# Routed experts of a two-block model: 127 blocks of 128 slots as split fp32r products, and 80 blocks of four quarters with an expert each as plain float32

## The chip, the cores and the metric

The kernel runs on one core of a Trainium2 chip. Its time is device microseconds (us) of one execution, launch to end; three executions of the kernel before stand behind the median below. TensorE (PE) multiplies, VectorE (DVE), ScalarE (ACT) and GpSimd (POOL) compute beside it, SyncE (SP) issues most DMAs. All data are float32; fp32r is a format that TensorE reads faster than float32 and that keeps fewer bits, so the kernel before splits operands into a high and a low part.

## The reference

Two blocks are computed one after the other: `first_block` (modulation, projection, two recurrent mixers, output projection, a mixture of experts) and `second_block`. What the change touches is the mixture of experts of the first block, for 1024 tokens of 1024 numbers, 64 experts of inner width 256, of which every token takes 8:

```python
def _swiglu(x, wg, wu, wd):
    return (jax.nn.silu(x @ wg) * (x @ wu)) @ wd

def _moe(h, router_w, router_b, wg, wu, wd, sg, su, sd):
    ...
    _, top_e = lax.top_k(sel, TOP_K)
    gate = jnp.take_along_axis(scores, top_e, axis=1)
    gate = gate / jnp.sum(gate, axis=-1, keepdims=True) * ROUTE_SCALE
    ...
    def step(out, inp):
        tok, gw, e = inp
        y = _swiglu(h[tok], wg[e], wu[e], wd[e]) * gw[:, None].astype(h.dtype)
        return out.at[tok].add(y), None
    routed, _ = lax.scan(step, jnp.zeros_like(h), (tok_buf, gate_buf, blk_e))
    return _swiglu(h, sg, su, sd) + routed
```

The result is `x = x + g2 * _moe(h2_lat)`, normalized; the second block starts from it.

## The kernel before

The program is a row of stages, each with one block of instructions for every engine. Four of them matter here, in this order.

**`output_route`** (about 1530 to 1740 us) multiplies by `w_out` in 8 tiles of 128 tokens, normalizes, and computes router scores and gates. Every token's row with its 64 gates is stored to `yn` in HBM. SyncE issues the stores of a tile in the loop around L1960.

**`shared_expert`** counts the choices of each expert, and gives each expert as many blocks of 128 slots as it needs. A table in HBM holds the token of each slot; L2295 fetches it, 128 slots to a partition, and it is turned into `slots`. `owner` holds the expert of each block, and `done`, for each expert, where its blocks start. The shared expert's result is stored to `total` in HBM.

**`routed_experts`** (1800 to 3097 us) takes 127 blocks (`USED`), as many as could be needed. Block j, expert e:
- GpSimd gathers the 128 token rows of block j+3 into `xg` (L2494) and scatters the result of block j-1 with an addition into `total` (L2503). A scatter waits for the one before it.
- TensorE turns the rows of block j+1 (8 transposes, L2526), multiplies block j by the gate and up weights of its expert (8 slices of 128 rows, each 512 columns, three fp32r products for each: high x high, high x low, low x high, L2559), then multiplies block j-1 by its down weights (`down`: 6 fp32r products L2541, 2 plain float32 ones L2542), then transposes the hidden values of block j (L2568).
- ScalarE makes the high parts of the weights (`w_high`, 4 of 128x1024 a block, L2585; `wd_high`, L2605) and of the rows (L2580), the silu (L2623), and the scaled result (L2610).
- VectorE makes the low parts by subtraction (L2649, L2656, L2643), the product `hid` (L2683), and the indices.
- SyncE loads an expert's gate and up weights (L2468, two DMAs of 1 MB into `exp_w`, a ring of 4 experts) when the expert four back in the ring has been split for the last time, and its down weights (L2472, 1 MB into `wd`, also a ring of 4) when that expert's last down product is done. All three loads of an expert stand in one row of the queue, three experts ahead of use:

```python
with sp.Fori(1, N_EXPERTS // WS) as i:
    for w in range(WS):
        blocks = sp.value_load(tb["done"][0:1, bass.ds(i * WS + (w - WS + 1), 1)], ...)
        sp.wait_ge(w_split, blocks * Q)
        first(i * WS + w, w)
        sp.wait_ge(y_ready, blocks + 1)
        second(i * WS + w, w)
```

The order on each engine is the order of the code; the first four blocks and the last three are written out, the rest is a loop of four blocks. Semaphores count steps.

**The first stage of the second block** (`pre_...`, from 3107 us) loads each of 8 tiles of `total` and of x (L3438, L3441), multiplies `total` by the gain (L3655), adds it to x (L3667), normalizes twice, and transposes the tile on TensorE (L3523); then it multiplies by its projection weights (L3510). SyncE stores the tile (L3473) and loads small parameters between the tiles (L3459, L3463).

## Time and profile before

| | us |
|---|---|
| median of 3 executions | 4236.89 |
| lowest and highest | 4229.92, 4244.08 |
| the profiled execution | 4234.69 |
| its span, first to last instruction | 4232.8 |

| engine | busy us | share of the span |
|---|---|---|
| TensorE, products | 3643.4 | 86% |
| TensorE, loads of the stationary operand | 2938.0 | 69% |
| VectorE | 2676.3 | 63% |
| ScalarE | 2044.4 | 48% |
| GpSimd | 907.3 | 21% |

The shares are means over stages with different limits. The largest groups are all in the routed experts: VectorE's subtraction for `w_low` (603.0 us in 512 instructions), ScalarE's rounding for `w_high` (510.9 us) and TensorE's three kinds of product (415.0, 404.1 and 404.0 us). TensorE's instructions overlap and their ends are modelled, so a period is read from start to start, not from busy times. The DMA queues moved 690.96 MB. The chain of waits that ended last covers only the final stage, 4% of the span, so it says nothing of the stages spoken of here.

### The profile page before, as it was taken

To read this page: it belongs to the slowest core of one execution; us is meant where nothing else is said; L and a number is where in the kernel's file an instruction comes from. 1 tells how busy PE (TensorE), PEld (TensorE's weight loads), DVE (VectorE), ACT (ScalarE), POOL (GpSimd) and SP (SyncE) were. 2 spreads that over 40 slices of the span, in tenths; PEclk is the share of its full clock that TensorE was granted. 3 is DMA by queue.
4 is the path that set the end of the run, shared out by engine and by line. 5 is a ranking of instruction groups with operands and counts; after the bars stand their busy time and mean duration, and the time that the engine had idled before them with its cause. 6 is when DMAs were issued, how large, how long until landed. Compare 5 with 4: busy or idle time off the path is not lost. (4 is left out here: it accounts for less than half of the span.)

```text
span 4232.8 us, 93615 instructions
## 1 busy us (share of the span) xinstructions
PE 3643.4 (86%) x35448; PEld 2938.0 (69%) x35449; DVE 2676.3 (63%) x4120; ACT 2044.4 (48%) x2837; POOL 907.3 (21%) x799
## 2 busy tenths in 40 slices
PE   4899799678776679799999999999949989968779
PEld 0898788577676557377777677777737767856667
DVE  2588688555555566287777777777768666036731
ACT  1477576322222153077777777777742222136720
POOL 3000000134433003323223233322213333300000
PEclk6899899799899789899999999999969999989989
DMA  8254344322210635499999999754563421355552
GB/s 302 76 172 155 116 159 153 128 68 56 81 54 9 216 136 138 154 318 270 277 342 341 341 338 340 190 108 108 111 168 90 119 75 60 110 139 134 131 169 80
DMA packets 527112, 690.96 MB, mean 163 GB/s; under 512 B 77904, under 2 KB 424656, under 8 KB 523728
## 3 DMA queue, kind: packets, MB, share of 16 engines
q1 hardware_dynamic: 487232, 545.70, 40.5%
q0 software_dynamic: 39088, 139.12, 13.4%
q8 instruction: 240, 3.93, 0.4%
q10 hardware_dynamic: 480, 1.62, 0.1%
q14 instruction: 72, 0.59, 0.0%
HBM read 508.35 MB, written 178.00 MB: 162 GB/s over the span
## 5 line engine op out<-in xcount | busy, mean ns | idle before, releaser
L2649 DVE TENSOR_TENSOR routed_w_low<-moe_exp_w,routed_w_high 128x1024 fp32r<-128x1024 f32 x512 | 603.0, 1219 | 26.8 <-ACT routed_w_high L2585 23.5
L2585 ACT CAST routed_w_high<-moe_exp_w 128x1024 fp32r x512 | 510.9, 1045 | 61.7 <-DMA moe_exp_w<-in_exp_w_up_dram 26.0
L2503 POOL DMA_INDIRECT total<-routed_y,routed_yidx x127 | 238.0, 1874 | 825.6 <-ACT routed_y L2610 304.4
L2559 PE MATMUL routed_p_gu<-routed_w_high,routed_x_high 128*128 128x512 f32 x1016 | 415.0, 408 | 0.0
L2559 PE MATMUL routed_p_gu<-routed_w_low,routed_x_high 128*128 128x512 f32 x1016 | 404.1, 398 | 0.0
L2559 PE MATMUL routed_p_gu<-routed_w_high,routed_x_low 128*128 128x512 f32 x1016 | 404.0, 398 | 0.0
L548 PE MATMUL front_ps<-front_a_high,front_w_high 128*128 128x320 f32 (+1 forms) x1120 | 363.5, 325 | 16.7 <-DVE front_w_low L785 13.5
L548 PE MATMUL front_ps<-front_a_high,front_w_low 128*128 128x320 f32 (+1 forms) x1120 | 355.2, 317 | 0.0
L548 PE MATMUL front_ps<-front_a_low,front_w_high 128*128 128x320 f32 (+1 forms) x1120 | 355.0, 317 | 0.0
L3510 PE MATMUL pre_ps<-pre_a_high,pre_w_high 128*128 128x512 f32 x720 | 287.7, 400 | 15.3 <-ACT pre_xb L3644 6.6
L3510 PE MATMUL pre_ps<-pre_a_low,pre_w_high 128*128 128x512 f32 x720 | 281.7, 391 | 0.0
L3510 PE MATMUL pre_ps<-pre_a_high,pre_w_low 128*128 128x512 f32 x720 | 281.7, 391 | 0.0
L2542 PE MATMUL routed_p_y<-routed_wd,routed_hT_rest 128*128 x508 | 260.2, 593 | 0.0
L1427 POOL TENSOR_TENSOR rwmix_TT<-rwmix_at,rw_mask 64x256 f32<-64x256 f32 (+1 forms) x60 | 43.4, 724 | 944.4 <-DVE rwmix_at L1328 938.5
L548 PEld LDWEIGHTS front_ps<-front_a_high,front_w_high 128*128 128x128 f32 x1120 | 214.3, 191 | 35.5 <-DVE front_w_low L785 18.1
L2559 PEld LDWEIGHTS routed_p_gu<-routed_w_high,routed_x_low 128*128 128x128 f32 x1016 | 192.1, 189 | 46.7
L2559 PEld LDWEIGHTS routed_p_gu<-routed_w_low,routed_x_high 128*128 128x128 f32 x1016 | 192.9, 190 | 41.0
L2559 PEld LDWEIGHTS routed_p_gu<-routed_w_high,routed_x_high 128*128 128x128 f32 x1016 | 192.9, 190 | 41.1
L548 PEld LDWEIGHTS front_ps<-front_a_low,front_w_high 128*128 128x128 f32 x1120 | 214.2, 191 | 1.3
L548 PEld LDWEIGHTS front_ps<-front_a_high,front_w_low 128*128 128x128 f32 x1120 | 213.9, 191 | 0.0
L2494 POOL DMA_INDIRECT moe_xg<-yn,moe_idx x128 | 157.8, 1233 | 104.5 <-DVE moe_idx L2638 53.7
L3510 PEld LDWEIGHTS pre_ps<-pre_a_high,pre_w_high 128*128 128x128 f32 x720 | 136.2, 189 | 48.7 <-issue 18.1
(556 smaller groups left out, 8362.3 us busy)
## 6 DMA issues: line engine op xcount, KB each, us to landing
moe_exp_w<-in_exp_w_gate_dram SPq DMA_DIRECT2D x64, 1024.0 KB, 14.4
moe_exp_w<-in_exp_w_up_dram SPq DMA_DIRECT2D x64, 1024.0 KB, 19.3
routed_wd<-in_exp_w_down_dram SPq DMA_DIRECT2D x64, 1024.0 KB, 15.5
front_wt<-in_w_in_dram SPq DMA_DIRECT2D x70, 512.0 KB, 4.3
mod_w<-in_w_mod_dram SPq DMA_DIRECT2D x24, 1024.0 KB, 18.1
pre_wt<-in_w_in_dram SPq DMA_DIRECT2D x44, 512.0 KB, 4.1
out_a<-mix SPq DMA_DIRECT2D x24, 512.0 KB, 4.4
proj<-pre_xv SPq DMA_DIRECT2D x16, 512.0 KB, 2.6
```

What stands on the lines that cost most here:

```text
L548: op = nc.tensor.matmul(ps[:, s % 2, c, 0:size], w_part[:, s % 2, k, :], a_part[:, k, first + c * size:first + (c + 1) * size], start=(k = ...
L1427: nc.gpsimd.tensor_tensor(combos(TT[u][:])[to, es], combos(at[u][:])[at_rows, es], mask(MASK_LEVEL, at_rows, es), ALU.mult)
L2494: nc.gpsimd.indirect_dma_start(xg[:, b % 2, :], None, yn, bass.IndirectOffsetOnAxis(ap=idx[b][:, :], axis=0))\
L2503: nc.gpsimd.indirect_dma_start(total, bass.IndirectOffsetOnAxis(ap=yidx[b % 2][:, :], axis=0), y[:, b % 2, :], None, compute_op=ALU.add).t ...
L2542: op = nc.tensor.matmul(p_y[:, h, :], hT_rest[:, :], wd[:, bass.ds(e % WS, 1), 1, cols], start=False, stop=True)
L2559: op = nc.tensor.matmul(p_gu[:, :], x_part, w_part[:, k, :], start=(k == 0 and i == 0), stop=(k == KD - 1 and i == 2))
L2585: nc.scalar.copy(w_high[:, q * KQ:(q + 1) * KQ, :].rearrange("p k m -> p (k m)"), wgu[:, bass.ds(e % WS, 1), q * KQ:(q + 1) * KQ].rearrang ...
L2649: nc.vector.tensor_tensor(w_low[:, at, :].rearrange("p k m -> p (k m)"), wgu[:, bass.ds(e % WS, 1), at].rearrange("p o k j m -> p (o k j m)"),
L3510: op = nc.tensor.matmul(ps[:, u, a:a + n], w_part[:, u, k, :], a_part[:, k, a:a + n], start=(k == 0 and j == 0), stop=(k == KD - 1 and j = ...
```

## The change

A block becomes a quad of four quarters (`QUARTER` = 32 slots); each quarter has an expert of its own (`owner` has an entry for each of the four places of a quad), and there are 80 quads (`QUADS`), as many as could be needed.

- TensorE multiplies in plain float32. For each slice of weights four matmuls stand in a row, one for each quarter: 32 columns of the rows as stationary operand, 512 columns of that quarter's expert's weights moving, the output in partitions 32s to 32s+31 of one PSUM bank (L2590 up, 8 groups; L2605 down, 4 groups). The first quarter reads the weights from the ring by a register; the others read from `fixed`, a ring of 4 places.
- ScalarE copies the second quarter's weights into `fixed` (6 copies of 128x1024 a quad), VectorE those of the third and fourth (12 copies). The roundings and subtractions go.
- Each quarter adds into a copy of `total` of its own: `total` has four parts of `PART` rows. The shared expert's result is in part 0; the other three are filled with zeros by SyncE in `output_route`.
- SyncE's order: `next_first` of expert e+3 waits for the last quad's up products of expert e-1, and `next_second` of expert e stands behind it.
- `shared_expert` computes four owners for each quad with four times as wide a comparison, 4 transposes and 4 gathers of the table where there was 1.
- The first stage of the second block loads four parts for each tile (`sums_of`), TensorE adds them as products with the identity into a PSUM bank (8 plain float32 products a tile), and VectorE multiplies by the gain from there (2 instructions of 128x512).

```diff
+                if 1 <= i < SPOTS:
+                    sp.dma_start(total[i * PART:i * PART + SEQ, :].rearrange("(p r) (a l) -> p (r a) l", p=P, l=P),
+                                 none[:].rearrange("p (o l) -> p o l", o=1).broadcast_to([P, SEQ * D // P // P, P])).then_inc(none_sent, 16)
...
-BLOCKS = SEQ * TOP_K // P + N_EXPERTS
-USED = (SEQ * TOP_K + (P - 1) * N_EXPERTS + N_EXPERTS - TOP_K) // P
+SPOTS = 4
+QUARTER = P // SPOTS
+QUADS = (SEQ * TOP_K + (QUARTER - 1) * N_EXPERTS + N_EXPERTS - TOP_K) // QUARTER // SPOTS + 1
+PART = SEQ + QUARTER
...
-            nc.gpsimd.indirect_dma_start(places[:, :], None, table.rearrange("(b l) c -> b (l c)", l=P),
-                                         bass.IndirectOffsetOnAxis(ap=row[:, :], axis=0)).then_inc(fetched, 16)
+            for j in range(SPOTS):
+                nc.gpsimd.indirect_dma_start(places[:, j * QUARTER:(j + 1) * QUARTER], None, table.rearrange("(b l) c -> b (l c)", l=QUARTER),
+                                             bass.IndirectOffsetOnAxis(ap=row[:, j:j + 1], axis=0)).then_inc(fetched, 16)
...
-        wgu = tb["exp_wgu"]
+        wgu = tb["exp_rows"]
         wd = st.sb("wd", [P, WS, MT, D])
-        w_high, w_low = (st.sb(n, [P, KD, 2 * D_EXPERT], F32R) for n in ("w_high", "w_low"))
+        fixed = st.sb("fixed", [P, R, SPOTS - 1, D])
         gate = st.sb("gate", [P, BS])
         idx = tb["idx"]
         yidx = [st.sb(f"yidx{u}", [P, 1], U32) for u in range(2)]
         xg = tb["xg"]
-        x_high, x_low = (st.sb(n, [P, 2, KD, P], F32R) for n in ("x_high", "x_low"))
+        x = st.sb("x", [P, 2, KD, P])
...
+        def up_step(j, c):
+            return j * STEP + c
+
+        def down_step(j, m):
+            return NB * STEP + m if ends(j) else j * STEP + (STEP + CH + m)
+
+        def place_of(b, c):
+            return (b * STEP + c) % R
+
+        def spot(s):
+            return slice(s * P // SPOTS, (s + 1) * P // SPOTS)
...
+            def next_first(e, at, w):
+                quad = sp.value_load(tb["done"][0:1, at], min_val=0, max_val=NB - 2)
+                sp.wait_ge(chunk_done, quad * STEP + CH)
+                first(e, w)
+
+            def next_second(e, at, w):
+                quad = sp.value_load(tb["done"][0:1, at], min_val=0, max_val=NB - 2)
+                sp.wait_ge(chunk_done, quad * STEP + 2 * STEP)
+                second(e, w)
+
+            def only(e):
+                return bass.ds(e, 1)
 
             for w in range(WS):
                 if w:
                     sp.sem_inc(second_loaded[w], 16)
                 second(w, w)
-            with sp.Fori(1, N_EXPERTS // WS) as i:
+            for e in range(WS, 2 * WS - 1):
+                next_first(e, only(e - WS + 1), e % WS)
+            with sp.Fori(1, N_EXPERTS // WS - 1) as i:
                 for w in range(WS):
-                    blocks = sp.value_load(tb["done"][0:1, bass.ds(i * WS + (w - WS + 1), 1)], min_val=1, max_val=NB)
-                    sp.wait_ge(w_split, blocks * Q)
-                    first(i * WS + w, w)
-                    sp.wait_ge(y_ready, blocks + 1)
-                    second(i * WS + w, w)
+                    next_first(i * WS + (w + WS - 1), only(i * WS + w), (w + WS - 1) % WS)
+                    next_second(i * WS + w, only(i * WS + (w - WS + 1)), w)
+            for e in range(N_EXPERTS - WS, N_EXPERTS):
+                if e + WS - 1 < N_EXPERTS:
+                    next_first(e + WS - 1, only(e), (e + WS - 1) % WS)
+                next_second(e, only(e - WS + 1), e % WS)
...
+            def copies(g):
+                pe.wait_ge(first_copied, g + 1)
+                pe.wait_ge(others_copied, g + 1)
+
+            def up(j, b):
+                e = owner(pe, j, 0)
+                pe.wait_ge(x_made, j + 1)
+                if not begins(j):
+                    pe.wait_ge(hid_made, j)
+                for c in range(CH):
+                    copies(up_step(j, c))
+                    for k in range(c * KC, (c + 1) * KC):
+                        cols = slice((k - c * KC) * BANK, (k - c * KC + 1) * BANK)
+                        for s in range(SPOTS):
+                            w = wgu[:, bass.ds(e % WS, 1), k * BANK:(k + 1) * BANK] if s == 0 else fixed[:, place_of(b, c), s - 1, cols]
+                            op = nc.tensor.matmul(p_gu[spot(s), :], x[:, b % 2, k, spot(s)], w, start=(k == 0), stop=(k == KD - 1))
+                    op.then_inc(chunk_done, 3 if begins(j) and c == CH - 1 else 1)
+
+            def down(j, b):
+                e = owner(pe, j, 0)
+                pe.wait_ge(hT_made, j + 1)
+                if not begins(j):
                     pe.wait_ge(y_made, j)
-                for h in range(2):
-                    cols = slice(h * BANK, (h + 1) * BANK)
-                    for i, (h_part, w_part) in enumerate(((hT_high, wd_high), (hT_high, wd_low), (hT_low, wd_high))):
-                        nc.tensor.matmul(p_y[:, h, :], h_part[:, :], w_part[:, cols], start=(i == 0), stop=False)
-                    op = nc.tensor.matmul(p_y[:, h, :], hT_rest[:, :], wd[:, bass.ds(e % WS, 1), 1, cols], start=False, stop=True)
-                op.then_inc(y_ready, 1)
-
-            pe.sem_inc(y_ready, 1)
+                for m in range(MT):
+                    copies(down_step(j, m))
+                    at = place_of(0, m) if ends(j) else place_of(b + 1, CH + m)
+                    for h in range(2):
+                        cols = slice(h * BANK, (h + 1) * BANK)
+                        for s in range(SPOTS):
+                            w = wd[:, bass.ds(e % WS, 1), m, cols] if s == 0 else fixed[:, at, s - 1, cols]
+                            op = nc.tensor.matmul(p_y[spot(s), h, :], hT[:, m, spot(s)], w, start=(m == 0), stop=(m == MT - 1))
+                    op.then_inc(chunk_done, 1)
+
...
+                if not ends(j):
+                    turn(j + 1, (b + 1) % BS, r + (b + 1) // BS)
+                up(j, b)
+                if not begins(j):
+                    down(j - 1, (b - 1) % BS)
...
+            def up_copy(e, j, b, c):
+                g = up_step(j, c)
+                if not isinstance(j, int) or g >= R:
+                    act.wait_ge(chunk_done, g - (R - 1))
+                nc.scalar.copy(fixed[:, place_of(b, c), 0, :],
+                               wgu[:, bass.ds(e % WS, 1), c * D:(c + 1) * D].rearrange("p o n -> p (o n)"))\
+                    .then_inc(first_copied, 3 if begins(j) and c == CH - 1 else 1)
+
+            def down_copies(j, b):
+                e, last = owner(act, j, 1), owner(act, j, SPOTS - 1)
                 for w in range(WS):
-                    act.wait_ge(second_loaded[w], (e + (WS - w)) // WS * 16 + (16 if w else 0))
-                if not isinstance(j, int) or j >= 1:
-                    act.wait_ge(y_ready, j + 1)
-                nc.scalar.copy(wd_high[:, :], wd[:, bass.ds(e % WS, 1), 0, :].rearrange("p o n -> p (o n)")).then_inc(down_rounded, 1)
+                    act.wait_ge(second_loaded[w], (last + (WS - w)) // WS * 16 + (16 if w else 0))
+                for m in range(MT):
+                    act.wait_ge(chunk_done, down_step(j, m) - (R - 1))
...
+            def up_copies(es, j, b, c):
+                g = up_step(j, c)
+                if c == 0:
+                    for w in range(WS):
+                        dve.wait_ge(loaded[w], (es[-1] + (WS - w)) // WS * 32 + (16 if w else 0))
+                if not isinstance(j, int) or g >= R:
+                    dve.wait_ge(chunk_done, g - (R - 1))
+                for s in (2, 3):
+                    op = nc.vector.tensor_copy(fixed[:, place_of(b, c), s - 1, :],
+                                               wgu[:, bass.ds(es[s] % WS, 1), c * D:(c + 1) * D].rearrange("p o n -> p (o n)"))
+                op.then_inc(others_copied, 3 if begins(j) and c == CH - 1 else 1)
+
+            def down_copies(j, b):
+                es = owner(dve, j, 2), owner(dve, j, 3)
+                for w in range(WS):
+                    dve.wait_ge(second_loaded[w], (es[1] + (WS - w)) // WS * 16 + (16 if w else 0))
+                for m in range(MT):
+                    dve.wait_ge(chunk_done, down_step(j, m) - (R - 1))
+                    at = place_of(0, m) if ends(j) else place_of(b + 1, CH + m)
+                    for s, e in zip((2, 3), es):
+                        op = nc.vector.tensor_copy(fixed[:, at, s - 1, :], wd[:, bass.ds(e % WS, 1), m, :].rearrange("p o n -> p (o n)"))
+                    op.then_inc(others_copied, 1)
+
+            def place(j, b, r):
                 if not isinstance(j, int) or j >= 2:
...
+            def sums_of(t):
+                for j in range(SPOTS):
+                    sp.dma_start(parts_t[t % 2][j], total[j * PART + t * P:j * PART + (t + 1) * P, :]).then_inc(parts_ready[t % 2], 16)
...
+                if t + 2 < LAT_TILES:
+                    sp.wait_ge(summed, t + 1)
+                    sums_of(t + 2)
...
+            def sums_of(t):
+                pe.wait_ge(parts_ready[t % 2], 16 * SPOTS * (t // 2 + 1))
+                if t >= 1:
+                    pe.wait_ge(part_made, t)
+                for a in range(2):
+                    for j in range(SPOTS):
+                        op = nc.tensor.matmul(ps[:, a, BANK:2 * BANK], consts["ident"][:, :], parts_t[t % 2][j][:, a * BANK:(a + 1) * BANK],
+                                              start=(j == 0), stop=(j == SPOTS - 1))
+                op.then_inc(summed, 1)
+
+            sums_of(0)
             for t in range(LAT_TILES):
+                if t + 1 < LAT_TILES:
+                    sums_of(t + 1)
...
-                dve.wait_ge(x_ready[t % 4], 32 * (t // 4 + 1))
-                nc.vector.tensor_tensor(total_t[t % 4][:, :], total_t[t % 4][:, :], gain_row[:, :], ALU.mult).then_inc(part_made, 1)
+                dve.wait_ge(summed, t + 1)
+                for a in range(2):
+                    cols = slice(a * BANK, (a + 1) * BANK)
+                    op = nc.vector.tensor_tensor(spread[:, t % 2, cols], ps[:, a, BANK:2 * BANK], gain_row[:, cols], ALU.mult)
+                op.then_inc(part_made, 1)
```

On TensorE, in the loop of the routed experts: end of the down products of one block and the start of the next block's, before. `p_x`, `p_h`, `p_gu`, `p_y` are PSUM tiles of the turned rows, the turned hidden values, the up and the down products.

```order
L2541 MATMUL routed_p_y<-routed_wd_low,routed_hT_high 128x512
L2541 MATMUL routed_p_y<-routed_wd_high,routed_hT_low 128x512
L2542 MATMUL routed_p_y<-routed_wd,routed_hT_rest 128x512
L2568 MATMUL routed_p_h<-ident,routed_hid 128x128 x2
L2526 MATMUL routed_p_x<-ident,moe_xg 128x128 x8
L2559 MATMUL routed_p_gu<-routed_w_high,routed_x_high 128x512
L2559 MATMUL routed_p_gu<-routed_w_low,routed_x_high 128x512
L2559 MATMUL routed_p_gu<-routed_w_high,routed_x_low 128x512
```

The same place after:

```order
L2605 MATMUL routed_p_y<-routed_wd,routed_hT 32x512
L2605 MATMUL routed_p_y<-routed_fixed,routed_hT 32x512 x3
L2620 MATMUL routed_p_h<-ident,routed_hid 128x128 x2
L2571 MATMUL routed_p_x<-ident,moe_xg 128x128 x8
L2474 TENSOR_LOAD moe_owner
L2474 ISA x2
L2590 ISA
L2590 MATMUL routed_p_gu<-moe_exp_w,routed_x 32x512
L2590 MATMUL routed_p_gu<-routed_fixed,routed_x 32x512 x3
```

The order of the parts of a block is the same; a group of one matmul from the ring and three from `fixed` stands where three split products stood.

On SyncE, in its loop over the experts, before (`TENSOR_LOAD moe_done` reads where an expert's blocks end):

```order
L2480 TENSOR_LOAD moe_done
L2480 ISA x2
L2481 REGISTER_ALU
L2468 ISA
L2468 DMA moe_exp_w<-in_exp_w_gate_dram 128x8x256
L2468 DMA moe_exp_w<-in_exp_w_up_dram 128x8x256
L2483 REGISTER_ALU
L2472 DMA routed_wd<-in_exp_w_down_dram 128x2x1024
```

After:

```order
L2503 TENSOR_LOAD moe_done
L2503 ISA x2
L2504 ISA
L2496 ISA
L2496 DMA moe_exp_w<-in_exp_w_gate_dram 128x8x256
L2496 DMA moe_exp_w<-in_exp_w_up_dram 128x8x256
L2508 ISA
L2508 TENSOR_LOAD moe_done
L2508 ISA x2
L2509 ISA
L2500 ISA
L2500 DMA routed_wd<-in_exp_w_down_dram 128x2x1024
```

The two rows of L2496 are for the expert three later than the row of L2500 behind them; before, all three rows were for one expert, and the wait of `second` was for the same block as that of `first`.

## Rows read from the trace of the kernel before

**Rows 1.** Windows: us, busy per engine (x instructions), clock, DMA share, GB/s

```profile
core 0: us, PE busy (x) PEld busy (x) DVE busy (x) ACT busy (x) POOL busy (x), PEclk, DMA share, GB/s
1580.00:1700.00 120.00, 110.72 (x542) 89.58 (x541) 76.31 (x253) 41.15 (x57) 40.15 (x37) 0.93 0.47 130
...
2100.00:2600.00 500.00, 474.13 (x2083) 356.00 (x2081) 371.36 (x521) 360.56 (x475) 153.62 (x95) 0.99 1.07 340
2700.00:3000.00 300.00, 300.00 (x1349) 227.68 (x1348) 234.44 (x335) 229.70 (x305) 83.51 (x61) 1.00 0.50 110
...
3100.00:3160.00 60.00, 9.85 (x40) 7.84 (x40) 37.68 (x42) 24.29 (x38) 10.99 (x7) 0.50 0.71 211
```

**Rows 2.** Timeline of TensorE over one block: start, us, engine, line, names

```profile
2799.88 1.04 PE L2526 MATMUL routed_p_x<-ident,moe_xg 128*128 128x128 f32 x8
2800.67 0.48 PE L2559 MATMUL routed_p_gu<-routed_w_high,routed_x_high 128*128 128x512 f32 x1
...
2807.06 1.02 PE L2542 MATMUL routed_p_y<-routed_wd,routed_hT_rest 128*128 x2
...
2808.62 1.02 PE L2542 MATMUL routed_p_y<-routed_wd,routed_hT_rest 128*128 x2
2809.48 0.38 PE L2568 MATMUL routed_p_h<-ident,routed_hid 128*128 128x128 f32 x2
2809.70 1.04 PE L2526 MATMUL routed_p_x<-ident,moe_xg 128*128 128x128 f32 x8
```

**Rows 3.** The scatters: duration ns, first and last start, and landing

```profile
L2503 POOL DMA_INDIRECT total<-routed_y,routed_yidx x127: 1567/1585/3718, 1820.9 to 3096.0; - x127
...
DMA to landing us min/median/max: 5.9/8.9/11.5
```

**Rows 4.** Waits of 1850 to 3100: engine, line, waited for, us, times, longest

```profile
ACT routed_w_high L2585 <- DMA moe_exp_w<-in_exp_w_up_dram: 26.0, 14, 4.9
...
PE routed_p_x L2526 <- DMA moe_xg<-yn,moe_idx: 19.6, 18, 2.0
```

**Rows 5.** Timeline of TensorE in the modulation and state-space stages, narrow outputs

```profile
52.88 1.04 PE L257 MATMUL mod_ps<-mod_w,mod_act_c 128*2 128x512 f32 x8 [0.59 <-DMA mod_w<-in_w_mod_dram]
...
3940.60 1.95 PE L3141 MATMUL ssd_py<-ssd_xf,ssd_skip 128*128 128x128 f32 x16
3942.48 1.97 PE L3147 MATMUL ssd_py<-ssd_ce,ssd_s 128*64 128x128 f32 x32
3944.28 1.92 PE L3153 MATMUL ssd_py<-ssd_m,ssd_xdt 128*64 128x128 f32 x32
```

**Rows 6.** A one-source VectorE instruction within SBUF: ns min/median/max

```profile
L3734 DVE TENSOR_SCALAR pre_buf<-pre_buf x4: 693/694/695, 3376.4 to 3574.4; 128x1024 f32<-128x1024 f32 x4
```

**Rows 7.** Groups of 1850 to 3100: busy us, mean ns, idle before

```profile
L2649 DVE TENSOR_TENSOR routed_w_low<-moe_exp_w,routed_w_high 128x1024 fp32r<-128x1024 f32 x488 | 574.7, 1219 | 26.5 <-ACT routed_w_high L2585 23.3
L2585 ACT CAST routed_w_high<-moe_exp_w 128x1024 fp32r x488 | 486.9, 1045 | 58.7 <-DMA moe_exp_w<-in_exp_w_up_dram 26.0 <-issue 19.4 <-PE routed_p_gu L2559 11.4
...
L2610 ACT ACTIVATE routed_y<-routed_p_y,routed_gate 128x1024 f32<-128x1024 f32 x123 | 139.4, 1133 | 6.9 <-PE routed_p_y L2542 6.8
...
L2580 ACT CAST routed_x_high<-routed_p_x 128x1024 fp32r<-128x1024 f32 x122 | 124.8, 1023 | 14.7 <-PE routed_p_x L2526 14.6
...
L2683 DVE TENSOR_TENSOR routed_hid<-routed_sg,routed_p_gu 128x256 f32<-128x256 f32 x122 | 50.5, 414 | 1.1 <-ACT routed_sg L2623 1.1
...
L2623 ACT ACTIVATE routed_sg<-routed_p_gu 128x256 f32<-128x256 f32 x122 | 46.7, 383 | 2.2 <-PE routed_p_gu L2559 1.0
```

**Rows 8.** Loads of the down weights, L2472, 1 MB each: issue to landing

```profile
DMA to landing us min/median/max: 4.9/15.5/20.7
```

**Rows 9.** Timeline of the second block's first stage

```profile
3128.30 3.25 DVE L3671 TENSOR_TENSOR pre_xv<-pre_xb,pre_xc 128x1024 f32<-128x1024 f32 x1
...
3137.53 1.97 PE L3523 MATMUL pre_aux<-ident,pre_yb 128*128 128x128 f32 x8 [9.22 <-DVE pre_yb L3685]
...
3144.19 1.97 PE L3523 MATMUL pre_aux<-ident,pre_yb 128*128 128x128 f32 x8 [4.68 <-DVE pre_yb L3685]
...
3152.40 1.69 SPq L3463 DMA_DIRECT2D pre_lw<-in_lru_w_a_dram  x2
```

295 lines of the change are left out of this document (141 added, 154 removed).

## The prediction

> **What bounds the kernel now.** I read the windows first, to see whose time the expert stage is; then the timeline of TensorE over one block, for its period; then groups, waits and DMA rows, for what stands in the way of a shorter period; last the stretch behind the stage, which the change also touches.
>
> In a quiet part of the stage, 2700 to 3000 us, TensorE is busy for all 300.00 us at full clock, VectorE for 234, ScalarE for 230, and the DMA engines for half of the time at 110 GB/s [rows 1]. So TensorE sets the period: 2799.88 to 2809.70, 9.82 us [rows 2]. In 2100 to 2600 the DMA engines are full (share 1.07, 340 GB/s) and TensorE falls to 474 of 500 [rows 1]: weights of a new expert, 3.15 MB, come just in time or a little late. The scatters, 127 from 1820.9 to 3096.0, give a mean period of 10.12 [rows 3]. So 127 x 9.82 = 1247 us are products and some 38 us waits; the largest are 26.0 for weights and 19.6 for gathered rows [rows 4]. The reference's inputs are fixed, and counting its router's choices gives 93 blocks with tokens and 34 empty ones, which cost the same.
>
> **The change, the products.** A quad replaces a block. 80 quads stand for 127 blocks (the same count gives 288 quarters with tokens, 72 quads, and 8 empty). Per quad: 8 groups of four matmuls up, 4 groups of four down, 8 + 2 transposes. The 24 + 6 fp32r products and the 2 plain ones of a block go.
> A plain float32 product of 512 columns is two records: from 2808.62 to 2809.48, 0.86 us [rows 2]. Do four strips of 32 columns share that time? The modulation stage runs eight records, four plain products into four partition groups, in 1.04 us from first start to last end [rows 5]; one product alone has 1.02 from start to end [rows 2]. So four cost one. There they write different banks. The state-space stage writes two strips of 64 into one buffer: 32 records from 3942.48 to 3944.28, 56 ns each, against 16 in 1.88 us, 118 ns each, with the full width [rows 5]. So strips go beside each other in one bank too. I take 0.86 a group, with four different moving streams and stationary loads of 32 columns hidden as those of 64 are there.
> 12 x 0.86 = 10.3. The turn is 2799.88 to 2800.67, 0.8, and the two transposes 0.2 [rows 2]. For two owner reads and four changes of shape I add 0.6, bounds 0 and 1.5 (no row shows a change from full width to strips; the upper bound is half a turn and half a group each way, rounded up). Quad: **11.9 us**. 80 x 11.9 = 952, against 1247 + 38: **-333 us** (bounds -381 and -261).
>
> **The copies** have to fit under 11.9. VectorE: 12 copies of 128x1024 from SBUF to SBUF. The nearest row is 694 ns [rows 6]; the subtraction that they replace is 1219 with two sources [rows 7]. 12 x 0.694 = 8.3, the hid product 0.41 [rows 7], gates and indices below 1: 9.6 us. ScalarE: 6 x 1.045 = 6.3, result 1.13, silu 0.4, rows and h transposes 1.4: 9.2 us [rows 7]. The ring of four is refilled three steps ahead, 5 us of products, so both are hidden and cost nothing; were each copy 1.22, VectorE would need 16 us and set the period (rival D).
>
> **The down weights.** SyncE's queue changes order (the listing of the change shows it): gate and up weights of expert e+3 are issued first, then the down weights of e, and both stand behind the end of the up products of e-1's last quad. Before, all three of e were issued three experts ahead. So down weights now start 2.1 MB behind in the queue, when their expert is near. Where e begins in the quad in which e-1 ends, its first down comes one quad later: 11.9 us. What must land by then is 3.15 MB. Gathers and scatters move 110 GB/s x 9.82 = 1.08 MB a block [rows 1], 91 GB/s at 11.9 us; of 340 stay 249 GB/s: 12.6 us. Landing has a fixed part: 4.9 us at least for 1 MB, which at 340 takes 3.1 [rows 8], so some 1.8; then a copy of 1.3. 15.7 against 11.9: 3.8 us late. The count gives 43 such quads, in 6 of which two new experts follow (a second 12.6, of which earlier slack takes a third: 12 late). Of the other 37 I let half pay, since many start with a drained queue: 18.5 x 3.8 = 70, and 6 x 12 = 72: **+142** (bounds: 0, if the gathers rest while weights come, and 240, from all 37 and 16 each). Long stops also let the clock drop: where TensorE had 9.85 of 60 us it was 0.50 [rows 1], while short ones in 2100 to 2600 left 0.99: **+20** (0 to 60). Filling and draining a stage of longer steps: **+8**.
> Expert stage: -333 + 142 + 20 + 8 = **-163**.
>
> **The sum of parts, second block.** Per tile four loads of 512 KB, 8 plain products with the identity, two VectorE products from PSUM rather than one of 1.22. Before, tiles follow every 6.65 us (3137.53 to 3144.19), paced by VectorE, with the clock at 0.50 [rows 1, 9]. Eight plain products take 6.9 us at full clock and 13.8 at half; the sum of t+1 stands ahead of the transposes of t on TensorE, and waits for the product that empties its bank (1.4). That is 8.3 us; the loads for t+2 need 2.1 MB, 6.2 + 1.8 us, after the sum of t, and wait on SyncE behind the store of the tile before and small parameter loads (a pair took 1.69) [rows 9]. I take 11 us a tile once the clock is up: 8 x 4.35 = 35, and 22 for the first tile (six more loads ahead of it, cold products): **+57** (35 to 100).
> **Zeros**: 12.6 MB in the output stage, 37 us at 340 GB/s; the share is 0.47 there [rows 1] so most is hidden: **+5** (0 to 20). Three more transposes and three more gathers of the table: **+4**.
>
> **Sum**: -163 + 57 + 5 + 4 = **-97**. From the profiled execution's 4234.69 that gives 4138; the median shown is 2.2 above it: **4140 us**.
>
> **Rivals.**
> A. The down weights are late by half or less. For it: the weights' median landing of 15.5 us was under a full queue [rows 8], and empty quads and second quads of an expert let it drain. Against: 64 x 12.6 = 806 us of weights into 72 x 11.9 = 857, little slack. Half the +142 and none of the +20: 4049.
> B. Late weights cost 240 rather than 142 and the sums of parts 70: 4251. It needs the queue never to drain.
> C, the slower side. GpSimd is held up by VectorE's copies. The scatters are a chain, each waits for the last, which lands after 8.9 us (11.5 at most) [rows 3]. That VectorE and GpSimd hinder each other is in rows: at 3128.30 a VectorE product took 3.25 us for 1.22 with GpSimd busy [rows 9]. If GpSimd can write descriptors only between copies (8.3 of 11.9 us are copies), its 1.6 and 1.2 us of issue become 5.3 and 3.9: 8.9 + 3.7 + 3.9 = 16.5 us a quad, 1320 us in place of the forecast's 952 + 142 + 20 (weights are then in time): 4346. It decides from 15.2 us a quad, where the stage's gain is the 66 us that the rest costs. Against: scatters issued in 1.585 us (median) beside a VectorE busy for 78% [rows 1, 3], though with two-source work. The Trainium skill's page "SBUF — State Buffer" (section "The "DVE blocks DMA" trap", under "SBUF: two separate sides") speaks for this rival: float32 copies within SBUF lock GpSimd out, and it gives about 620 ns growing to 3100. By its figures the two issues would grow by 2.5 us each: 14 us a quad, 1120 us for the stage, which is the forecast's time with another cause; no row here shows such a copy beside a scatter.
> D. The copies take 1.22 us as other VectorE work [rows 7]: 12 x 1.22 + 2 = 16.6 us a quad, 1328: 4354. Against it the 694 ns [rows 6].
> E. Only two strips run at a time: 1.72 a group, 22.2 a quad; 824 more, less the 162 for late weights: 4802. Against: [rows 5]. The skill's "TensorE: Matmul & The Clock Gate" (Part 3: Packing small matmuls) gives 2.38 times for three column strips of 32, not 3: 0.86 x 3 / 2.38 = 1.08 a group by that, an estimate that would put 2.7 us on a quad; the modulation stage's 1.04 with its tail speaks for less.
> F. The change does not do what it says, and strips run one after another: 12 x 3.44 + 1.6 = 43 us a quad, 2490 more than 11.9 and 162 less for weights: 6470.
>
> **How the numbers follow.** Forecast 4140 (4090 to 4195 by itself) 0.50, A 0.27, B 0.10, C 0.08, D 0.02, E 0.02, F 0.01. Range: 4030 to 4255, which holds the forecast, A and B. 0.3%, 12.7 us, is what a measurement of this kernel can tell. Faster: 0.50 + 0.27 + 0.03 of B = 0.80; the same: 0.04 of B, 0.01 of C; slower: 0.15.
>
> **What would show it.** A period of 11.9 in the timeline of two empty quads at the end, and 0.86 from group to group. VectorE copies near 0.69. Late weights as ScalarE's or VectorE's copy of the down weights waiting for the DMA of the down matrix, TensorE's down line behind them, in quads where an expert begins. Tiles of the second block every 11 us, with the load of the parts last. Wrong would be: waits of TensorE for gathered rows and scatters landing over 12 us (C), groups of 1.1 us or more, or hardly any wait for down weights (A).

## The result, and the profile after

| kernel | median us | lowest, highest | runs |
|---|---|---|---|
| before | 4233.41 | 4228.34, 4257.26 | 6 |
| after | 4262.45 | 4251.84, 4275.09 | 6 |

The ratio is 1.0063, with a 95% interval of 1.0037 to 1.0089: the change makes the kernel slower, by 27 us by that ratio and by 29 by the medians. The forecast was 4140, 4030 to 4255. The profiled execution of after took 4251.84 us, its span is 4250.0.

The expert stage as a whole, windows of the kernel before and of the one after, from TensorE's first turn to the first load of the next stage (columns as in [rows 1]):

```profile
1794.07:3107.29 1313.22, 1264.07 (x5596) 953.44 (x5596) 992.23 (x1403) 967.09 (x1275) 395.84 (x255) 0.99 0.85 252
```

```profile
1803.40:3061.60 1258.20, 1006.23 (x8480) 335.05 (x8480) 680.49 (x1518) 685.37 (x800) 204.81 (x158) 0.90 0.74 222
```

The stage is 55 us shorter, where 163 were forecast. TensorE is busy for 1006 of 1258 us, with a mean clock of 0.90 against 0.99. The timeline of TensorE after, over one quad in the quiet tail, answers to [rows 2]:

```profile
2957.94 1.04 PE L2571 MATMUL routed_p_x<-ident,moe_xg 128*128 128x128 f32 x8
2958.91 0.62 PE L2590 MATMUL routed_p_gu<-moe_exp_w,routed_x 128*32 x1
...
2959.79 0.59 PE L2590 MATMUL routed_p_gu<-moe_exp_w,routed_x 128*32 x1
2959.80 0.61 PE L2590 MATMUL routed_p_gu<-routed_fixed,routed_x 128*32 128x512 f32 x3
2960.22 0.59 PE L2590 MATMUL routed_p_gu<-moe_exp_w,routed_x 128*32 x1
...
2969.62 1.04 PE L2571 MATMUL routed_p_x<-ident,moe_xg 128*128 128x128 f32 x8
```

Four strips start within 10 ns of each other, and the next four records follow after 0.43 us; a group of eight records takes 0.86. The quad takes 2969.62 - 2957.94 = 11.68 us, against 11.9 forecast. 80 quads are 934 us. So the stage has 1258 - 934 = 324 us of something else: 1258 - 1006 = 252 in which TensorE stands still, and 1006 - 934 = 72 in which its own instructions take longer than at full clock. The clock's part is seen in the timeline behind a stop:

```profile
2952.40 0.92 PE L2605 MATMUL routed_p_y<-routed_wd,routed_hT 128*32 x1 [3.62 <-DVE routed_fixed L2724]
...
2953.11 1.06 PE L2605 MATMUL routed_p_y<-routed_wd,routed_hT 128*32 x1
...
2953.96 1.06 PE L2605 MATMUL routed_p_y<-routed_wd,routed_hT 128*32 x1
...
2955.67 0.76 PE L2605 MATMUL routed_p_y<-routed_wd,routed_hT 128*32 x1
2955.69 0.76 PE L2605 MATMUL routed_p_y<-routed_fixed,routed_hT 128*32 128x512 f32 x3
2956.26 0.59 PE L2605 MATMUL routed_p_y<-routed_wd,routed_hT 128*32 x1
```

After 3.62 us without work the steps are 0.85 us (1.2 GHz) from 2953.11 to 2955.67, and then 0.43 again (2.4 GHz). What TensorE waits for stands in the waits of 1800 to 3150, which answer to [rows 4]:

```profile
ACT routed_fixed L2655 <- DMA routed_wd<-in_exp_w_down_dram: 266.3, 29, 19.6
PE routed_p_y L2605 <- DVE routed_fixed L2724: 229.0, 33, 16.5
DVE routed_fixed L2724 <- DMA routed_wd<-in_exp_w_down_dram: 188.0, 25, 18.6
```

TensorE waits 229 us for copies of down weights, 33 times, up to 16.5 us. VectorE and ScalarE in turn wait for the down matrix. That is the forecast mechanism, larger than forecast. But 33 is not the 43 quads of the count, and VectorE's own wait for the DMA is 41 us short of TensorE's. The groups show that there is more. Copies and scatters after:

```profile
L2712 DVE COPY routed_fixed<-moe_exp_w 128x1024 f32 x640 | 402.7, 685 | 27.5 <-PE routed_p_y L2605 21.8
...
L2547 POOL DMA_INDIRECT total<-routed_y,routed_yidx x80 | 127.0, 1587 | 903.3 <-ACT routed_y L2661 868.6
...
L2701 DVE COPY routed_gate<-moe_xg 32x1 f32 x320 | 46.5, 145 | 218.5 <-issue 151.1
```

A copy takes 685 ns, as [rows 6] let expect, a scatter's issue 1587 ns on average, as the median before [rows 3]. New is the last row: VectorE stands 151 us before its gate copies with nothing that it waits for ("issue"). The timeline of VectorE, and under it the records of the loop's own line, of one place:

```profile
2432.48 3.69 DVE L2712 COPY routed_fixed<-moe_exp_w 128x1024 f32 x6
2445.55 0.62 DVE L2701 COPY routed_gate<-moe_xg 32x1 f32 x4 [9.38 <-issue]
```

```profile
L2461 DVEq COMPARE_BRANCH  x1: 62/62/62, 2434.4 to 2434.4; - x1
...
L2461 ACTq COMPARE_BRANCH  x1: 45/45/45, 2434.5 to 2434.5; - x1
L2461 ACTq FUSED_REGOPS  x1: 50/50/50, 2434.8 to 2434.8; - x1
...
L2461 DVEq FUSED_REGOPS  x1: 85/85/85, 2441.4 to 2441.4; - x1
```

L2461 is the loop over the quads. ScalarE's branch back at 2434.5 is followed by its next instruction at 2434.8. VectorE's branch at 2434.4 is followed by its next at 2441.4: 7 us in which its sequencer has no instruction; the copies that it had already handed out end at 2436.2. The loop has 18 passes, so 17 branches back (the expectations below say 18). Over these 17 the gap has a median of 6.34 us and sums to 89; in the kernel before it is 0.23 each time. Counted in the trace, a pass of VectorE's loop has 303 to 305 instructions after and 134 before.

TensorE's long stops before down products (those over 1 us) fall into two groups: 17 end 11 to 20 us after one of these 17 branches and take 113 us together, and 16 stand elsewhere and take 123. In the second group down weights are late; in the first the gap has its part, and what part is for the experiments to show.

The page's rows on instruction fetches, before and after, fit:

```profile
q14 instruction: 72, 0.59, 0.0%
```

```profile
q14 instruction: 162, 1.33, 0.1%
```

90 more packets, 5 for each of 18 passes. Their times fit too: in each of the 17 gaps one or two packets of the instruction queue start (at 2436.2 and 2439.4 in the gap shown). How long the gap is goes with what the DMA engines do. The 7 us behind the branch at 2434.4, and behind the one at 2940.9, whose gap is 2.72 us (columns as in [rows 1]):

```profile
2434.42:2441.42 7.00, 7.00 (x68) 2.52 (x69) 1.75 (x3) 2.93 (x4) 1.58 (x1) 1.00 1.04 352
2941.00:2948.00 7.00, 7.00 (x68) 2.52 (x69) 2.30 (x7) 4.96 (x6) 1.58 (x1) 1.00 0.32 39
```

Ten of the 17 gaps are 6.2 to 7.1 us, all with a DMA share of 1.03 or more behind the branch; the other seven are 2.7 to 4.3 us, with 0.38 or less.

Outside the stage. It began 9.4 us later (1803.4 for 1794.07), but that is a difference of two things. The code up to the output stage is the same in both kernels, and took 1537.3 us in this execution and 1555.9 in the one before: 19 us of scatter (1537 to 1556 over the runs of this document that leave it as it is). From the first product of the output stage to TensorE's first turn, before and after:

```profile
1555.95:1794.07 238.12, 206.54 (x803) 140.48 (x803) 114.01 (x348) 53.17 (x70) 69.21 (x68) 0.92 0.53 162
```

```profile
1537.34:1803.44 266.10, 213.84 (x805) 146.06 (x806) 115.72 (x351) 52.86 (x70) 71.16 (x71) 0.89 0.68 193
```

+28 us. This stretch hardly scatters: 235.8 to 239.7 us in the four runs of the kernel before and its variants, 262.6 to 270.5 in the eight of the changed kernel that write the zeros in the output stage. From the first product of the shared expert to the first turn, where the owners are computed, it is 68.7 us against 68.5, so all of the 28 stand ahead of that. ScalarE's wait for the rows of `mix` in the output stage grows from 25.1 us (1540 to 1800, before) to 72.3 (1530 to 1804, after):

```profile
ACT out_a_high L2069 <- DMA out_a<-mix: 72.3, 7, 20.0
```

The second block's first stage took 106.0 us from its first load to its first projection product (3061.64 to 3167.64) in place of 53.9 (3107.29 to 3161.19), +52. TensorE there, after:

```profile
3073.98 9.55 PE L3601 MATMUL pre_ps<-pre_buf,ident 128*128 128x512 f32 x16 [25.13 <-DMA pre_buf<-total]
3085.07 7.10 PE L3601 MATMUL pre_ps<-pre_wide,ident 128*128 128x512 f32 x16 [1.55 <-DVE pre_wide L3752]
3094.99 1.10 PE L3617 MATMUL pre_aux<-ident,pre_yb 128*128 128x128 f32 x8 [2.81 <-DVE pre_yb L3784]
3099.65 8.66 PE L3601 MATMUL pre_ps<-pre_buf,ident 128*128 128x512 f32 x16 [3.56 <-DMA pre_buf<-total]
...
3128.37 9.66 PE L3601 MATMUL pre_ps<-pre_buf,ident 128*128 128x512 f32 x16 [5.45 <-DMA pre_buf<-total]
...
3154.98 1.10 PE L3617 MATMUL pre_aux<-ident,pre_yb 128*128 128x128 f32 x8 [2.77 <-DVE pre_yb L3784]
```

The sum of one tile takes 7.0 to 10.2 us, and every other one waits for the loads of the parts. From the transposes of the first tile (3094.99) to those of the fifth (3154.98) a tile takes 15.0 us on average, against 6.65 before [rows 9]; the first projection product follows the fifth tile in both kernels.

### The profile page after: what moved, and what is told of

Read it like the earlier page. It is cut to its first block and busy times, and to the rows that moved or that the text cites. A ratio compares the mean times of both kernels' runs of the same rounds, so it can differ in the third digit from the quotient of the medians.

```text
span 4250.0 us, 100490 instructions
## 1 busy us (share of the span) xinstructions
PE 3448.2 (81%) x38463; PEld 2344.2 (55%) x38464; DVE 2362.7 (56%) x4246; ACT 1762.9 (41%) x2362; POOL 718.8 (17%) x706
## 5 line engine op out<-in xcount | busy, mean ns | idle before, releaser
L2590 PE MATMUL routed_p_gu<-routed_fixed,routed_x 128*32 128x512 f32 x3840 | 567.0, 595 | 0.0
L2590 PE MATMUL routed_p_gu<-moe_exp_w,routed_x 128*32 x1280 | 565.9, 595 | 0.7 <-DVE routed_fixed L2712 0.7
L2605 PE MATMUL routed_p_y<-routed_wd,routed_hT 128*32 x640 | 349.6, 698 | 236.4 <-DVE routed_fixed L2724 229.0
L2644 ACT COPY routed_fixed<-moe_exp_w 128x1024 f32 x320 | 333.8, 1046 | 247.8 <-PE routed_p_y L2605 150.5
L2712 DVE COPY routed_fixed<-moe_exp_w 128x1024 f32 x640 | 402.7, 685 | 27.5 <-PE routed_p_y L2605 21.8
L2724 DVE COPY routed_fixed<-routed_wd 128x1024 f32 x320 | 200.1, 688 | 306.2 <-DMA routed_wd<-in_exp_w_down_dram 188.0
L2605 PE MATMUL routed_p_y<-routed_fixed,routed_hT 128*32 128x512 f32 x1920 | 350.5, 698 | 0.0
L2605 PEld LDWEIGHTS routed_p_y<-routed_wd,routed_hT 128*32 128x32 f32 x640 | 76.8, 126 | 487.9 <-issue 487.0
L2590 PEld LDWEIGHTS routed_p_gu<-moe_exp_w,routed_x 128*32 128x32 f32 x1280 | 134.4, 110 | 350.7 <-issue 350.7
L2655 ACT COPY routed_fixed<-routed_wd 128x1024 f32 x160 | 164.5, 1045 | 297.3 <-DMA routed_wd<-in_exp_w_down_dram 266.3
L2547 POOL DMA_INDIRECT total<-routed_y,routed_yidx x80 | 127.0, 1587 | 903.3 <-ACT routed_y L2661 868.6
## 6 DMA issues: line engine op xcount, KB each, us to landing
routed_wd<-in_exp_w_down_dram SPq DMA_DIRECT2D x64, 1024.0 KB, 12.6
```

The lines of the kernel that those rows point to most:

```text
L2547: nc.gpsimd.indirect_dma_start(total, bass.IndirectOffsetOnAxis(ap=yidx[b % 2][:, :], axis=0), y[:, b % 2, :], None, compute_op=ALU.add).t ...
L2590: op = nc.tensor.matmul(p_gu[spot(s), :], x[:, b % 2, k, spot(s)], w, start=(k == 0), stop=(k == KD - 1))
L2605: op = nc.tensor.matmul(p_y[spot(s), h, :], hT[:, m, spot(s)], w, start=(m == 0), stop=(m == MT - 1))
L2644: nc.scalar.copy(fixed[:, place_of(b, c), 0, :], wgu[:, bass.ds(e % WS, 1), c * D:(c + 1) * D].rearrange("p o n -> p (o n)"))\
L2655: nc.scalar.copy(fixed[:, at, 0, :], wd[:, bass.ds(e % WS, 1), m, :].rearrange("p o n -> p (o n)"))\
L2712: op = nc.vector.tensor_copy(fixed[:, place_of(b, c), s - 1, :], wgu[:, bass.ds(es[s] % WS, 1), c * D:(c + 1) * D].rearrange("p o n -> p ( ...
```

## Experiments

Each ratio below is to the kernel before, with its 95% interval.

**Theory 1**: the order of loads on SyncE makes down weights late. Rivals: bandwidth (3.15 MB an expert do not fit), or something else altogether. The edit for `lag1`, in the loop over the experts (and alike in its first and last steps):

```diff
-                    next_first(i * WS + (w + WS - 1), only(i * WS + w), (w + WS - 1) % WS)
+                    next_first(i * WS + (w + 1), only(i * WS + (w + -2)), (w + 1) % WS)
                     next_second(i * WS + w, only(i * WS + (w - WS + 1)), w)
```

> Down weights of expert e are issued after the gate and up weights of e+1 rather than of e+3; same bytes, same products. Theory 1 (the order on SyncE's queue): the changed kernel's expert stage, 1258 us of which 934 are products (80 x 11.68), loses 236 us to down weights issued too late and some 70 us to the clock that drops in those waits. With the earlier issue the stage falls to 1000 to 1080 us, TensorE waits under 60 us on down weights, the clock is back above 0.96 there, and the time is 4060 to 4090. Rival (bandwidth: 3.15 MB an expert do not fit into what gathers and scatters leave): the wait moves from down to gate and up weights, the stage stays above 1180 us, the time above 4190.

Measured: 4145.79 us, 0.9777 (0.9753 to 0.9802). The waits of 1800 to 2950:

```profile
PE routed_p_y L2605 <- DVE routed_fixed L2724: 109.3, 18, 8.2
...
DVE routed_fixed L2724 <- DMA routed_wd<-in_exp_w_down_dram: 33.6, 15, 2.6
```

117 us came back by moving one load, at the same bytes, so the order, and not the bandwidth, made these down weights late. But the expectation failed in its size: 190 us were expected, and TensorE still waits 109 us, 18 times, while VectorE's wait for the matrix itself has all but gone. Of the 18 waits 17 are over 3 us, and each of them ends 11.5 to 16.0 us after one of the 17 branches back.

`lag2`, with 2 in place of 1:

> The same with the down weights of e behind the gate and up weights of e+2. Theory 1: between the two: the issue is one expert earlier than in the changed kernel, which is enough for nearly all, 4080 to 4150. Rival (bandwidth): above 4190 as the changed kernel. If it equals the run with e+1, one expert of lead is enough.

Measured: 4150.98, 0.9791 (0.9773 to 0.9808), 5 us from `lag1` and within the two intervals: one expert of lead is nearly enough.

`nodown` leaves the load itself out:

```diff
-                sp.dma_start(wd[:, w], routed[2][bass.ds(e, 1)]...).then_inc(second_loaded[w], 16)
+                if isinstance(e, int) and e < WS:
+                    sp.dma_start(wd[:, w], routed[2][bass.ds(e, 1)]...).then_inc(second_loaded[w], 16)
+                else:
+                    sp.sem_inc(second_loaded[w], 16)
```

> Down weights are loaded for the first four experts only and never again (this leaves 60 of the 64 loads of 1 MB out, so the results of later experts are of wrong weights); products, copies and waits otherwise as in the changed kernel. It bounds what both order and bandwidth can give: stage 950 to 1000 us, clock above 0.97, time 3970 to 4010. If the stage is clearly longer than 1000 us, something else than down weights keeps TensorE from its 11.68 us a quad.

Measured: 4126.26, 0.9729 (0.9704 to 0.9753), where 3970 to 4010 was expected. Its waits of 1800 to 2950:

```profile
PE routed_p_y L2608 <- DVE routed_fixed L2727: 112.2, 18, 7.8
```

With no down weights to wait for TensorE still waits 112 us for VectorE's copy of them, 18 times, and again 17 of these are over 3 us and end 11.5 to 15.6 us after a branch back. So something else than down weights holds about half of the loss, as the expectation's last sentence let expect.

`onepart` puts the old first stage of the second block back, on part 0 alone:

```diff
-                for j in range(SPOTS):
-                    sp.dma_start(parts_t[t % 2][j], total[j * PART + t * P:j * PART + (t + 1) * P, :])...
+                sp.dma_start(parts_t[t % 2][0], total[t * P:(t + 1) * P, :]).then_inc(parts_ready[t % 2], 16)
...
-            sums_of(0)
...
-                if t + 1 < LAT_TILES:
-                    sums_of(t + 1)
...
+                nc.vector.tensor_tensor(spread[:, t % 2, :], parts_t[t % 2][0], gain_row[:, :], ALU.mult)...
```

> The second block's first stage reads part 0 of the sums only (one load a tile, multiplied by VectorE from SBUF as in the kernel before); parts 1 to 3 are left out of the result. From first load to first projection product 106 us in the changed kernel, 54 before. If the sum of parts is the cause: 54 to 60 us, and the time 4205 to 4215. If the loads of x or the order on SyncE had made the difference: above 70 us and 4225.

Measured: 4217.33, 0.9956 (0.9937 to 0.9975). First load to first product is 3069.8 to 3130.5, 60.7 us against 106.0: the sum of parts costs 45 us. The remaining 7 over the 53.9 of the kernel before are not explained by it.

**Theory 2**: VectorE's loop body is too long, and each branch back costs it a fetch. `flat` writes VectorE's loop out:

```diff
-            turns(dve, body)
+            for j in range(NB):
+                body(j, j % BS, j // BS)
```

> VectorE's loop over the quads is written out (80 bodies, no branch back); all else as in the changed kernel. In its trace VectorE stands still 6.34 us (median) after each of 18 branches back, 89 us in all, where the kernel before has 0.23; its body has 303 instructions a pass against 134. Theory 2 (a loop body of 303 instructions costs VectorE a fetch at each pass, and TensorE then waits for its copies): no such gap, and the time falls by 60 to 110 us to 4150 to 4200, since late down weights stay. Rival (VectorE's gap is covered by the late weights or by the ring of copies): within 20 us of 4262.

Measured: 4196.66, 0.9922 (0.9893 to 0.9951), 66 us less than after, as expected. Its waits of 1809 to 3011, where the late down weights are alone:

```profile
PE routed_p_y L2605 <- DVE routed_fixed L2724: 185.8, 25, 18.2
```

`flat_lag1` has both edits:

> Both: VectorE's loop written out, and the down weights of e issued behind the gate and up weights of e+1. In the run with the earlier issue alone TensorE still waited 109 us for VectorE's copies, 18 times, once a pass. Theory 2: these go, the clock in the stage rises above 0.97, the stage is 960 to 1020 us, the time 3990 to 4040. Rival (the rest is the clock or bandwidth): above 4100.

Measured: 4021.36, 0.9497 (0.9482 to 0.9513), 241 us less than after, where the two edits alone gave 117 and 66. The stage in windows, `lag1`, `flat` and `flat_lag1`:

```profile
1817.40:2952.70 1135.30, 988.05 (x8480) 333.95 (x8480) 679.10 (x1518) 687.74 (x800) 204.61 (x158) 0.92 0.81 246
```

```profile
1809.00:3011.10 1202.10, 996.74 (x8480) 335.61 (x8480) 680.87 (x1518) 684.88 (x800) 209.86 (x159) 0.91 0.77 232
```

```profile
1816.50:2831.30 1014.80, 948.19 (x8480) 332.79 (x8480) 682.47 (x1518) 683.84 (x800) 215.81 (x159) 0.97 0.89 275
```

| | stage | TensorE still | busy over 934 (clock) |
|---|---|---|---|
| after | 1258 | 252 | 72 |
| `lag1` | 1135 | 147 | 54 |
| `flat` | 1202 | 205 | 63 |
| `flat_lag1` | 1015 | 67 | 14 |

The two edits together give more than the sum of each, in both columns. As long as one kind of stop stays, the mean clock stays at 0.91 to 0.92; only with both gone is it 0.97. The waits of `flat_lag1` in 1800 to 2900 show what most of its 67 us are:

```profile
DVE routed_fixed L2712 <- DMA moe_exp_w<-in_exp_w_up_dram: 64.2, 12, 22.2
...
PE routed_p_h L2620 <- DVE routed_hid L2753: 47.0, 12, 20.4
```

VectorE's copies wait 12 times for gate and up weights, and TensorE 12 times for `hid`, which stands behind such copies in VectorE's order. So something of the bandwidth rival is left once the rest is gone: weights that come late whatever their order, for some 47 us.

How long may a body be? The kernel before, with VectorE's loop as eight blocks a pass:

```diff
+                with eng.Fori(0, NB // BS // 2) as i:
+                    for b in range(2 * BS):
+                        body(i * (2 * BS) + (BS + b), b % BS, i * 2 + (1 + b // BS))
```

> The kernel before with VectorE's loop of four blocks written as a loop of eight, 15 passes in place of 30, some 262 instructions a pass; nothing else differs. Theory 2: the gap after VectorE's branch grows from 0.23 us to about 6, 15 times; VectorE has about 2 us of slack a block, so 40 to 60 us slower, 4280 to 4300. If the gap stays at 0.23: a body of 262 instructions still fits, and the limit lies between it and 303, or the length is not the cause.

Measured: 4230.02, 0.9985 (0.9972 to 0.9998). The gap is 0.23 us, at 262 instructions a pass. Of the expectation's two branches the first, 6 us, failed; the second held: 262 still fit, or the length is not the cause. With twelve blocks a pass:

> The kernel before with VectorE's loop written as twelve blocks a pass, 10 passes, some 395 instructions a pass (four blocks: 134; eight blocks gave 262 instructions and a gap of 0.23 us). If the length of the body is the cause of the gap: 6 us after each of 9 branches back, up to 40 us slower. If it stays at 0.23, the gap of the changed kernel has another cause than length.

Measured: 4257.98, 1.0057 (1.0035 to 1.0079), 24 us slower. The loop's records in 2430 to 2545:

```profile
L2456 DVEq COMPARE_BRANCH  x1: 63/63/63, 2448.6 to 2448.6; - x1
L2456 DVEq FUSED_REGOPS  x1: 85/85/85, 2454.5 to 2454.5; - x1
```

5.8 us here, a median of 5.48 over the 9 branches back, 389 instructions a pass. The six of them with a DMA share of 0.90 to 1.06 behind the branch have 5.4 to 6.0 us, the last three, with 0.31 to 0.48, have 2.7 to 2.8. Last, the changed kernel with the loop kept and the body shortened, and earlier down weights:

```diff
-                    for w in range(WS):
-                        dve.wait_ge(loaded[w], (es[-1] + (WS - w)) // WS * 32 + (16 if w else 0))
+                    dve.wait_ge(first_copied, g + 1)
...
-                es = owner(dve, j, 2), owner(dve, j, 3)
-                for w in range(WS):
-                    dve.wait_ge(second_loaded[w], (es[1] + (WS - w)) // WS * 16 + (16 if w else 0))
+                es = (known.get(b) or (None, None, owner(dve, j, 2), owner(dve, j, 3)))[2:]
+                dve.wait_ge(first_copied, down_step(j, 0) + 1)
...
```

> Earlier down weights (behind e+1), and VectorE's loop kept, with 265 instructions in its listing instead of 301: it waits for ScalarE's copy of the same weights in place of four waits on the loads, and keeps two quads' owners in registers. If the limit lies between 262 and 303 instructions: the gap is gone or partly, time 4020 to 4060, near the version without a loop (4021). If not, it stays within 20 us of the 4146 of the earlier down weights alone.

Measured: 4018.57, 0.9487 (0.9463 to 0.9510), the same as without a loop. Its loop records in 2425 to 2475:

```profile
L2461 DVEq COMPARE_BRANCH  x1: 56/56/56, 2470.4 to 2470.4; - x1
L2461 DVEq FUSED_REGOPS  x1: 85/85/85, 2470.7 to 2470.7; - x1
```

265 to 273 instructions a pass and a gap of 0.23 us (0.27 once), with no packet of the instruction queue in any of the 17; the page counts 76 such packets, against 162 after. `before_u8` and `before_u12`, which differ in nothing but the blocks in a pass, have 73 and 119. So the gap is a fetch of instructions, and the length of the body decides on it, between 273 and 303 instructions. Where a body lies among the instructions may decide too; no run varied that alone.

One part of the change alone, its order on SyncE, in the kernel before:

> The kernel before with the changed kernel's order on SyncE: gate and up weights of e+3 issued ahead of the down weights of e. One part of the change alone. Theory 1 (this order makes down weights late): ScalarE waits over 100 us for the down matrix and the time rises by 60 to 150 us. Rival (only the shorter quads make them late): within 20 us of the kernel before.

Measured: 4256.68, 1.0051 (1.0034 to 1.0068), some 22 us slower. ScalarE waits for the down matrix in this kernel's waits of 1850 to 3100:

```profile
ACT routed_wd_high L2618 <- DMA routed_wd<-in_exp_w_down_dram: 80.7, 28, 4.7
```

The theory's 60 to 150 us are far off, and the rival's bound of 20 is narrowly missed: the order makes down weights late here too, but less (4.7 us at most), and most of it is absorbed. The full price needs the quads.

Zeros written in the stage of the recurrent mixer, in its SyncE loop (the lines in the output stage go):

```diff
+                if n == UNITS - 1:
+                    sp.wait_ge(none_made, 1)
+                    for i in range(1, SPOTS):
+                        sp.dma_start(total[i * PART:i * PART + SEQ, :]..., none[:]...).then_inc(none_sent, 16)
```

> The changed kernel with the three copies of zeros (12.6 MB) written in the recurrent mixer's stage and not in the output stage. In the profile the expert stage began 9.4 us later than before. If the zeros are the cause: 5 to 12 us less than the changed kernel, 4250 to 4257. If they were hidden: within 3 us of 4262.

Measured: 4258.40, 1.0051 (1.0033 to 1.0069), 4 us from after: within the noise. The profile shows why it is so little. From the first product of the output stage to the first turn it is now

```profile
1567.66:1806.90 239.24, 207.44 (x806) 140.69 (x806) 115.57 (x352) 53.26 (x71) 72.59 (x71) 0.92 0.56 162
```

239 us in place of 266: the zeros are the whole of the 28 there. But the mixer's stage, from its first product to that of the next, now takes 606.1 us, and 605.5 in `combo2`, against 576.4 to 591.3 in the other twelve runs. So the zeros were moved and hardly saved: they cost some 20 us where they are now. They are issued at 1259.7, and in 1250 to 1300 the DMA share is 0.87 and TensorE is busy for 33.7 of 50 us at a clock of 0.80, where after has 0.02, 41.1 us and 0.97.

Everything together: the two edits of `flat_lag1`, the moved zeros, and one edit more on SyncE: the parts of tile t+3 are loaded right behind the store of tile t (and those of tile 2 ahead of the loop):

```diff
-                if t + 2 < LAT_TILES:
-                    sp.wait_ge(summed, t + 1)
-                    sums_of(t + 2)
                 sp.wait_ge(h_made, t + 1)
                 sp.dma_start(h[t * P:(t + 1) * P, :], x_t[t % 4]).then_inc(h_sent[t % 4], 16)
+                if t + 3 < LAT_TILES:
+                    sp.wait_ge(summed, t + 2)
+                    sums_of(t + 3)
```

> Both of these, and two more: the three copies of zeros are written in the recurrent mixer's stage, where the DMA share is 0.02 to 0.04, instead of the output stage; and in the second block's first stage SyncE issues the four loads of tile t+3 right behind the store of tile t, ahead of x and the small parameters. Expected: 9 us less for the zeros, 15 to 25 for the order: 3960 to 4010. If zeros had no price: under 3 us.

Measured: 3989.60, 0.9435 (0.9418 to 0.9452), the fastest version here. From first load of the parts to first product it takes 2820.0 to 2906.3, 86.3 us, in place of 108.9 in `flat_lag1` (2831.3 to 2940.2): 23 us for the order. The other 9 of the 32 us below `flat_lag1` are what moving the zeros gives, 29 in the output stage less 18 in the mixer's stage, within the scatter.

## Why the prediction was wrong

- **Products**: right. 11.9 a quad was forecast, 11.68 measured. Four strips share the time of one. Rivals E and F fall.
- **Copies**: the duration was right (0.694 forecast, 0.685 measured), and D falls. The step that failed is that they "are hidden and cost nothing". VectorE's 9.6 us of work did fit; its instructions did not. The listing has 301 in the loop where there were 131, and I summed the time of the copies and never the length of the loop. The gap of 6.34 us (median), at each of 17 branches back, was in no term and in no rival. Taking it out alone gives 66 us (`flat`), and with the earlier down weights already in place 124 (`lag1` to `flat_lag1`).
- **Late down weights**: the mechanism was right. With VectorE's loop written out, in order not to mix the two, TensorE waits 186 us for copies of down weights in 25 stops, where 142 in some 25 were forecast: the count was right, and a stop lasts 7.4 us and not 5.8. The earlier issue then takes the idle time from 205 to 67 us. That this is 138, close to the 142, is luck: 47 us of waits behind gate and up weights come in its place.
- **Clock**: forecast +20, measured 72. I took long stops only, from the windows; the timeline shows that 3.62 us without work are enough for 3 us at half speed. With 33 stops for copies alone this is a large term.
- **Zeros and table**: forecast +5 and +4, measured 28 and 0. That the zeros are mostly hidden was the second step that failed: a DMA share of 0.47 left room, but with them ScalarE's wait for `mix` grew by 47 us, and `zearly` shows that without them the 28 us are gone from the stage. In the two profiles the stage starts only 9.4 us later, as forecast; that is luck, since the code ahead happened to take 19 us less.
- **The next stage**: forecast +57, measured +52, of which `onepart` returns 45. The way there was wrong in part: 11 us a tile were forecast for eight tiles, and it is 15.0 between the five that stand ahead of the first product; the first tile's transposes come 33.4 us after the first load in place of 19.1, +14 where 22 were forecast.
- **The stage as a whole**: -163 from 1313 would have been 1150 us; it is 1258, 108 more. The products take 18 less than forecast, the clock 52 more, and TensorE stands still for 74 more than the late weights and the filling of the forecast.
- **Rival B** comes nearest in number (4251) and is not what happened: idle time was as large as it said, but a good part of it was the gap, and the DMA share of the stage is 0.74, so the queue does drain. **Rival A** falls. **Rival C** falls, though not by the scatters of this run: they land after a median of 6.3 us (8.9 before [rows 3]), but 78 of the 80 are issued where VectorE makes no wide copy. In `short_lag1` 29 are issued beside such copies for 0.5 us or more and take 1.96 us (median; 2.24 at most) in place of 1.58, and 41 of 80 gathers stand beside them for over 0.9 us and take 1.06 in place of 0.97: slower, but nowhere near the 5.3 and 3.9 of C. The Trainium skill's page "SBUF — State Buffer" (section "SBUF: two separate sides") let expect that float32 copies within SBUF lock GpSimd out of writing descriptors; these runs show no more than these tenths of a microsecond. The 14 us a quad that the prediction works out from the page leave out the gather's own 1.2 us; added up as C's own sum, that estimate is 15.1.

The sum by what was measured in the two profiles: -19 of scatter in the code ahead of the output stage, +28 in the output stage, -55 in the routed experts, +52 behind them, and +11 in all that follows (1082.4 us from the first projection product to the end, 1071.6 before): +17, the difference of the two spans. Of the last 11, 7.0 us are the sum of one more tile that stands behind the first projection product (3174.39); but `onepart`, which has no such sum, takes 1079.3 too, so the cause is open. The other runs of the kernel before take 1074.8 to 1076.4 there, those of the changed one 1075.8 to 1088.1. Without the scatter ahead the change costs some 30 us, as the medians say.

## What to carry to other kernels

When a change makes a loop body longer, count the body's instructions on each engine, register arithmetic and loads included, besides their time; an engine with time to spare can still stand for 3 to 7 us at each branch back. To price a term in a stretch, measure between two marks inside one execution: when a stage begins also holds the scatter of all that ran before it, here 19 us. Before a load is moved in a queue, ask what it stands behind and how long before its use it is issued; one expert of lead was worth over 100 us at the same bytes. Stops of a few microseconds cost TensorE twice, once in waiting and once in the clock behind them, so two causes of stops removed together gave more than the sum of each.
